# Hybrid encoder trunk, one core: squares, root and convolution gate placed inside the input projection, nine of twelve groups of branch transposes placed inside the linear attention, one gate product placed at its tail

## The chip, the cores and the metric

The kernel runs on one core of one Trainium2 chip. The metric is the device time of one execution in microseconds. The profile that is read below is one execution of the kernel before.

## What is computed

Two layers run over 768 tokens (a group of 512 and one of 256), all float32. Each layer starts with four mixers that share one input projection; then come an expert-choice mixture of experts and a gated input embedding, which the change leaves alone.

```python
def mixer_block(h, w_in, ...):
    u = h @ w_in                                   # 2592 columns for the mixers, 4096 for the gates
    qa = axial_rope(rmsnorm(qa, qk_g[0]), ...); ka = axial_rope(rmsnorm(ka, qk_g[1]), ...)
    oa = global_attention(qa, ka, va)
    ob = conv_module(ub, ...)                      # z = a * sigmoid(g), depthwise convolution, norm, silu
    oc = window_attention(rope(qc), rope(kc), vc, sink)
    od = gla_mixer(qd, kd, vd, rd, zlr, g2, gb2, gn)   # gated linear attention, rmsnorm, * silu(rd)
    gates = sigmoid(gates.reshape(B, S, 4, D_MODEL))
    merged = 0.0
    for i, o in enumerate((oa, ob, oc, od)):
        merged = merged + gates[:, :, i] * (o @ w_branch[i])
    return merged @ w_out
```

## The kernel before

Tokens lie in six tiles of 128. A float32 operand of a product is split into a high part (ScalarE copies it to fp32r: `hi`, `gate_hi`, `t_hi`, lines 714, 724, 746) and a low part (VectorE subtracts: `lo`, `gate_lo`, `t_lo`, lines 997, 1002, 1007), and TensorE makes three products of them. The order on each engine is written out by hand, as one program per engine; engines wait for each other through counting semaphores. Each queue is strictly in order, so a waiting instruction holds back all behind it.

A layer's mixer part runs in these stages.

- **Projection.** Six chunks of 432 columns, four weight steps each (`chunk`, `w_chunk`, lines 1433 to 1435). ScalarE empties a chunk into `u` (line 767) when TensorE has finished it. Chunk 0 holds the queries and keys of the global attention, chunks 1 and 2 the convolution's halves `UB` and `UG`.
- **Gates.** The 4096 gate columns are 32 products of 48 matmuls each (`gate_step`, line 1462), numbered f, which fill TensorE where a mixer would leave it waiting. Each needs its weights loaded (SyncE, line 475), split into `fhi` and `flo`, and its result copied out (`gate_out`, line 732) and stored to `gate_logits` (line 485).
- **Rope.** VectorE squares the queries and keys and sums them (lines 1053, 1055), ScalarE takes the sigmoid of `UG` and the root (795, 797), VectorE multiplies `UB` by it (1059), inverts the root (1076), rotates tile by tile into `rA` (1083 to 1097), GpSimd does the same for the window attention into `rC` (619 to 627). TensorE transposes both (1504), ScalarE copies the result out (807 to 809) and VectorE takes the low parts (`qk_lo`, 1068, 1071). Gate product t stands ahead of tile t's transposes, gate 0 ahead of all. Then the convolution input is transposed (1517).
- **Attention and convolution**, then **linear attention** in two passes over the tiles with a scan between. In the first pass a tile has a transpose of the low-rank columns (1578), products with the decay (1582, 1585), a product with `w2b` (1590), gate product `F_GLA + n`, and the key-value products (1601). In the second it has products 1618, half a gate product, 1630, the other half, 1648 and 1657, and twelve transposes (1669). `s_h[7]` tells that VectorE has masked `att` (1242), `s_h[8]` that 1648/1657 are done.
- **Tail.** The sixth tile's output is normalised (`oss`, `od4`, lines 902, 1280, 1282), then all branch outputs are transposed, twelve groups of four (1415), each group followed by `t_hi` and `t_lo` in two PSUM banks; between the sixth and the seventh group the first four branch weights are split.
- **Branches and merge.** Eight column blocks g, four branch products i each (line 1462 again), the gates' sigmoid on ScalarE (915), the product with it on VectorE (1301), the sum on GpSimd (645 to 651). Product i of block g waits for VectorE's product i of block g-1, which frees its banks.

SyncE's queue around the tail, before: after the last gate store it waits for all stores, loads the eight branch weights (493), waits for the normalised output and loads the gates of blocks 0 and 1 (503). `fout[0]` shares its memory with `raw[3]`, and `fhi`/`flo` share theirs with `raw[4]` to `raw[7]`.

## Time and profile before

| what | value |
|---|---|
| runs | 3266.78, 3263.78, 3262.92 us; median 3263.78 us |
| profiled execution | 3267.64 us, its span 3265.8 us |
| TensorE busy | 2936.4 us, 90% of the span |
| VectorE busy | 1973.6 us, 60% |
| ScalarE busy | 1679.0 us, 51% |
| GpSimd busy | 352.3 us, 11% |
| mean granted TensorE clock | 0.932 of full speed |
| TensorE's share of the chain that ended last | 72% |

The span runs from the first to the last instruction. The granted clock has two levels, 1.2 and 2.4 GHz, so 1.00 means 2.4 GHz throughout. An idle time of an engine, in brackets in a timeline, names who ended it. The two layers are alike: layer 1's projection lies at 51 to 218 us, layer 2's at 1662 to 1834 us.

### The profile page before, as it was taken

What the parts mean: (1) busy time and instruction counts of PE and PEld (TensorE: products, weight loads), DVE (VectorE), ACT (ScalarE), POOL (GpSimd) and SP (SyncE); (2) the same over time, 40 slices, a digit from 0 to 9 for tenths busy, and PEclk for the clock granted to TensorE, in tenths of its full rate; (3) what the DMA queues carried; (4) which work ended last, traced back from release to release, by engine and by line L of the source; (5) the groups of instructions that cost most, each with busy time, mean ns of one, the idle gap of its engine ahead of it and who ended that gap; (6) DMA issues with size and microseconds to landing.
All of it is one profiled execution on the core that took longest, in us unless ns stands there. A gap on an engine that the chain in (4) does not pass through costs nothing.

```text
span 3265.8 us, 45051 instructions
## 1 busy us (share of the span) xinstructions
PE 2936.4 (90%) x15468; PEld 2376.2 (73%) x15468; DVE 1973.6 (60%) x2548; ACT 1679.0 (51%) x2320; POOL 352.3 (11%) x362
## 2 busy tenths in 40 slices
PE   5989989989869999996979899899896999999966
PEld 4988877868746666664779888788685666666655
DVE  2135872447378888885231559533564788888833
ACT  3223335234258888885232333452332788888832
POOL 2012000006001011011010200000240011011010
PEclk9999989979879999997979999899896999999978
DMA  5112112137289999995131121121565899999832
GB/s 190 49 32 85 57 56 69 55 100 244 110 302 373 375 371 373 375 373 172 55 102 33 54 75 57 57 80 38 144 215 194 309 372 373 375 371 373 310 132 86
DMA packets 378229, 617.78 MB, mean 189 GB/s; under 512 B 20448, under 2 KB 141376, under 8 KB 377984
## 3 DMA queue, kind: packets, MB, share of 16 engines
q1 hardware_dynamic: 356080, 539.69, 47.7%
q0 software_dynamic: 20304, 70.21, 7.3%
q10 hardware_dynamic: 1728, 6.29, 0.5%
q8 instruction: 76, 1.25, 0.2%
q14 instruction: 41, 0.34, 0.0%
HBM read 553.20 MB, written 62.91 MB: 189 GB/s over the span
## 4 chain that ended last, share of the span: by engine, by line
PE 72%; ACT 9%; DVE 8%; issue 5%; DVEq 3%; DMA 2%; ACTq 1%; POOL 0%; POOLq 0%
PE PS L1462 18%; PE PS L1433 14%; PE PS L1435 14%; PE PS L1434 13%; ACT whi L714 5%; PE PS L1415 3%; DVE wlo L997 1%; PE PS L1553 1%; DVE zacc L1121 1%; PE PS L1704 1%; ACT L947 1%; ACT L714 1%; PE PS L1648 1%; DVE rows L1019 1%; PE PS L1618 1%
## 5 line engine op out<-in xcount | busy, mean ns | idle before, releaser
L997 DVE TENSOR_TENSOR wlo<-raw,whi 128x1024 fp32r<-128x1024 f32 (+2 forms) x880 | 1024.2, 1206 | 602.8 <-ACT whi L714 596.7
L714 ACT ACTIVATE whi<-raw 128x1024 fp32r<-128x1024 f32 (+2 forms) x880 | 886.2, 1036 | 502.5 <-PE PS L1435 485.7
L1462 PE MATMUL PS<-hT,fhi 128*128 128x512 f32 (+1 forms) x2048 | 460.1, 347 | 13.6 <-ACT fout L732 8.0
L1433 PE MATMUL PS<-whi,xeT 128*96 128x512 f32 x1024 | 411.9, 402 | 12.8 <-DVE wlo L997 10.3
L1435 PE MATMUL PS<-whi,xeT 128*96 128x512 f32 x1024 | 405.4, 396 | 0.0
L1434 PE MATMUL PS<-wlo,xeT 128*96 128x512 f32 x1024 | 403.5, 394 | 0.0
L1433 PE MATMUL PS<-whi,hT 128*128 128x432 f32 (+1 forms) x960 | 362.7, 378 | 17.3 <-DVE rows L1399 9.1
L1462 PEld LDWEIGHTS PS<-hT,fhi 128*128 128x128 f32 x2048 | 324.2, 193 | 73.3 <-issue 27.3
L1434 PE MATMUL PS<-wlo,hT 128*128 128x432 f32 (+1 forms) x960 | 360.1, 375 | 0.0
L1435 PE MATMUL PS<-whi,hT 128*128 128x432 f32 (+1 forms) x960 | 359.9, 375 | 0.0
L1462 PE MATMUL PS<-hT,flo 128*128 128x512 f32 (+1 forms) x1024 | 268.5, 344 | 0.0
L1433 PEld LDWEIGHTS PS<-whi,xeT 128*96 128x96 f32 x1024 | 165.8, 162 | 102.0 <-DVE wlo L997 34.4
L1435 PEld LDWEIGHTS PS<-whi,xeT 128*96 128x96 f32 x1024 | 166.1, 162 | 72.8
L1434 PEld LDWEIGHTS PS<-wlo,xeT 128*96 128x96 f32 x1024 | 166.6, 163 | 66.5
L1433 PEld LDWEIGHTS PS<-whi,hT 128*128 128x128 f32 x960 | 183.8, 191 | 42.6 <-issue 14.3
L1433 PE MATMUL PS<-whi,hidT 128*96 128x512 f32 x512 | 207.4, 405 | 0.0
L1435 PE MATMUL PS<-whi,hidT 128*96 128x512 f32 x512 | 201.5, 394 | 0.0
L1434 PE MATMUL PS<-wlo,hidT 128*96 128x512 f32 x512 | 201.0, 393 | 0.0
L1435 PEld LDWEIGHTS PS<-whi,hT 128*128 128x128 f32 x960 | 183.5, 191 | 20.0
L1434 PEld LDWEIGHTS PS<-wlo,hT 128*128 128x128 f32 x960 | 184.0, 192 | 18.9
L1462 PEld LDWEIGHTS PS<-hT,flo 128*128 128x128 f32 x1024 | 159.7, 192 | 23.4
L832 ACT ACTIVATE P<-PS,nm 128x256 f32<-128x256 f32 (+2 forms) x96 | 54.1, 563 | 177.5 <-DVE nm L1138 95.4
(273 smaller groups left out, 3967.2 us busy)
## 6 DMA issues: line engine op xcount, KB each, us to landing
raw<-in_w_gate_e SPq DMA_DIRECT2D x256, 512.0 KB, 10.5
raw<-in_w_up_e SPq DMA_DIRECT2D x256, 512.0 KB, 10.8
raw<-in_w_down_e SPq DMA_DIRECT2D x256, 512.0 KB, 11.2
raw<-in_w_in SPq DMA_DIRECT2D x64, 512.0 KB, 4.3
raw<-in_w_in SPq DMA_DIRECT2D x48, 432.0 KB, 3.3
rows<-x_res POOLq DMA_DIRECT2D x36, 512.0 KB, 8.3
x_res<-rows POOLq DMA_DIRECT2D x30, 512.0 KB, 4.3
gate_logits<-raw SPq DMA_DIRECT2D x32, 384.0 KB, 2.7
```

The lines of the kernel that those rows point to most:

```text
L714: A(whi[slot % SPLIT][:, 0:w], raw[slot][:, 0:w], ACT.Copy).then_inc(s_hi, 1)
L832: A(P[:, n % 2, 0:nk * 128], PS[:, n % 2, 0:nk * 128], ACT.Exp, bias=nm[:, n:n + 1], accum_out=sm[:, n:n + 1]).then_inc(s_p, 1)
L947: A(sil[:, c * 512:(c + 1) * 512], PS[0:CAP, c, :], ACT.Silu).then_inc(s_sil, 1)
L997: V.tensor_tensor(wlo[j % SPLIT][:, 0:w], raw[j % slots][:, 0:w], whi[j % SPLIT][:, 0:w].bitcast(F32), ALU.subtract).then_inc(s_lo, 1)
L1019: V.scalar_tensor_tensor(rows[:, t, :], rows[:, t, :], rs[:, t:t + 1], gain[:], ALU.mult, ALU.mult).then_inc(s_xn, 1)
L1121: V.scalar_tensor_tensor(zacc[:, c, :], z, cw[:, c, k:k + 1], zacc[:, c, :], ALU.mult, ALU.add).then_inc(s_conv, 1)
L1415: m = nc.tensor.transpose(PS[:, 6 + b, n * np_:(n + 1) * np_], x, ident[0:np_, 0:np_])
L1433: nc.tensor.matmul(out, x[0], w[0], start=first, stop=False)
L1434: nc.tensor.matmul(out, x[0], w[1], start=False, stop=False)
L1435: return nc.tensor.matmul(out, x[1], w[0], start=False, stop=last)
L1462: m = nc.tensor.matmul(PS[:, bb, 0:(t1 - t0) * 128], w[wn], x[xn](t0, t1), start=first and p == 0, stop=last and p == 2)
L1553: mm = nc.tensor.matmul(PS[:, 4 + (m // 4) % 2, h * HD:(h + 1) * HD], PT[:, m % 2, k * 128:(k + 1) * 128], u[:, k0 + k, v0:v0 + HD], start ...
```

## The change

1. The squares and sums of the queries and keys are made by VectorE after chunk 1's weight steps (scratch in `rA`), the root by ScalarE after chunk 1, the sigmoid of `UG` after chunk 2, and the inverse and the product with `UB` by VectorE after chunk 3's steps. The projection loops of ScalarE and VectorE are unrolled for this. TensorE's loop stays.
2. The gate product ahead of the sixth rope tile is left out there. All later products move one number down (`F_Z` is 5), and number 31, `F_TAIL`, is made at the end of the second pass: its first quarter behind 1630 of the last tile, the rest behind the first two transposed groups of the fourth branch.
3. The transposes are grouped anew (`T_UNITS`): six groups `AB` (one tile, two branches), three `C` and three `D` (two tiles, one branch). The nine groups AB and C run in the first pass of the linear attention, one behind the gate product of each tile, a second behind the key-value products of each odd tile, all in PSUM bank 3. The decays' products move from bank 3 to bank 0, behind the product with `w2b`.
4. At the tail the output of tiles 0 to 3 is normalised early (`od_norm(0, 4)`), and three groups are left, in banks 4, 3 and 5.
5. SyncE loads three branch weights and block 0's gates ahead of the last gate store, block 1's gates behind it, and the fourth to eighth branch weights after those.

The diff, cut to its core:

```diff
-F_ROPE, F_Z, F_ATT, F_CONV, F_GLA, F_SCAN, F_GLB = 0, 6, 8, 17, 19, 25, 26
+F_ROPE, F_Z, F_ATT, F_CONV, F_GLA, F_SCAN, F_GLB, F_TAIL = 0, 5, 7, 16, 18, 24, 25, 31
...
 T_N0, T_G, T_N1 = 0, 12, 24
+T_UNITS = [("AB", 0), ("AB", 1), ("C", 0), ("AB", 2), ("AB", 3), ("C", 1), ("AB", 4), ("AB", 5), ("C", 2),
+           ("D", 0), ("D", 1), ("D", 2)]
...
+        def branch_units(n):
+            return [k for k, (kind, m) in enumerate(T_UNITS)
+                    if (kind == "AB" and m == n) or (kind == "C" and 2 * m + 1 == n)]
+        def branch_bank(k):
+            kind, m = T_UNITS[k]
+            return PS[:, (4, 3, 5)[m] if kind == "D" else 3, :].rearrange("p (k n) -> p k n", n=256)
+        def branch_src(k, h):
+            kind, m = T_UNITS[k]
+            if kind == "AB":
+                return [ublk[:, m, b, 0, h * 128:(h + 1) * 128] for b in (0, 1)]
+            return [ublk[:, t, 2 if kind == "C" else 3, 0, h * 128:(h + 1) * 128] for t in (2 * m, 2 * m + 1)]
...
+                def load_branch(g):
+                    sp.wait_ge(s_lo, l * SPL + (S_G + g + 1))
...
+                def load_gates(g):
+                    for i in range(NB):
+                        if g >= 2:
+                            sp.wait_ge((s_mg, s_ga1, s_ga2, s_mg)[i], l * 8 + (g - 1))
+                        sp.dma_start(gates[g % 2][:, i], g_d[g * NB + i].rearrange("p (t n) -> p t n", n=128)
...
+                    if f == NF - 1:
+                        sp.wait_ge(s_flo, l * NF + NF)
+                        for g in range(FRAW):
+                            load_branch(g)
+                        sp.wait_ge(s_fout[0], l * (8 * NF) + 8 * NF)
+                        sp.wait_ge(s_fout[1], l * (8 * NF) + 8 * NF - 16)
+                        sp.wait_ge(s_h[8], l * NT + NT)
+                        load_gates(0)
...
-                wait_alone(sp, s_flo, l * NF + NF)
-                wait_alone(sp, s_fused, l * NF + NF + FSPLIT)
+                sp.wait_ge(s_fused, l * NF + NF + FSPLIT)
+                sp.wait_ge(s_od, 2 * l + 2)
+                load_gates(1)
                 for n in range(2):
-                    wait_alone(sp, s_fout[n], l * (8 * NF) + 8 * NF)
-                for g in range(8):
...
-                for g in range(10):
+                    sp.wait_ge(s_fout[n], l * (8 * NF) + 8 * NF)
+                for g in range(FRAW, 8):
+                    load_branch(g)
+                for g in range(2, 10):
...
-                with act.Fori(0, 2) as i:
-                    for j in range(2):
-                        w_chunk(i * 2 + j, 4 * j, True)
-                w_chunk(4, 0, True)
+                for ck in range(5):
+                    w_chunk(ck, 4 * (ck % 2), True)
+                    if ck == 1:
+                        act.wait_ge(s_ssq, l + 1)
+                        A(rqk[:], rqk[:], ACT.Sqrt, bias=eps64[:]).then_inc(s_rqk, 1)
+                    if ck == 2:
+                        act.drain()
+                        for t in range(NT):
+                            A(u[:, t, UG:UG + 256], u[:, t, UG:UG + 256], ACT.Sigmoid).then_inc(s_zs, 1)
...
-                    A(u[:, t, UG:UG + 256], u[:, t, UG:UG + 256], ACT.Sigmoid).then_inc(s_zs, 1)
-                act.wait_ge(s_ssq, l + 1)
-                A(rqk[:], rqk[:], ACT.Sqrt, bias=eps64[:]).then_inc(s_rqk, 1)
-                for t in range(NT):
-                    gate_hi(l, t + 1)
-                    gate_out(l, t)
+                    if t < NT - 1:
+                        gate_hi(l, t + 1)
+                        gate_out(l, t)
...
+                def branch_hi(k):
+                    t_hi(l * TPL + (T_G + k), branch_dst(k, 1), branch_bank(k))
...
+                        for k in branch_units(n):
+                            branch_hi(k)
...
-                    if t < NT - 1:
-                        gate_hi(l, F_GLB + t + 1)
+                    gate_hi(l, F_GLB + t + 1)
...
-                act.wait_ge(s_oss, l + 1)
-                A(oss[:], oss[:], ACT.Sqrt, bias=eps64[:]).then_inc(s_or, 1)
-                for c in range(2):
-                    if c == 1:
-                        act.wait_ge(s_od, l + 1)
-                        for n in range(4):
-                            hi(l * SPL + (S_G + n), n, 1024, R_G)
-                    for t in range(NT):
-                        t_hi(l * TPL + (T_G + 6 * c + t), urblk[:, t, 2 * c:2 * c + 2, 1, :],
-                             PS[:, 6 + t % 2, :].rearrange("p (k n) -> p k n", n=256))
+                act.wait_ge(s_oss, 2 * l + 1)
+                A(oss[:, 0:4], oss[:, 0:4], ACT.Sqrt, bias=eps64[:]).then_inc(s_or, 1)
+                branch_hi(9)
+                branch_hi(10)
+                act.wait_ge(s_oss, 2 * l + 2)
+                A(oss[:, 4:6], oss[:, 4:6], ACT.Sqrt, bias=eps64[:]).then_inc(s_or, 1)
+                act.wait_ge(s_h[8], l * NT + NT)
+                hi(l * SPL + S_G, 0, 1024, R_G)
+                branch_hi(11)
+                hi(l * SPL + (S_G + 1), 1, 1024, R_G)
+                hi(l * SPL + (S_G + 2), 2, 1024, R_G)
+                gate_out(l, F_TAIL)
+                hi(l * SPL + (S_G + 3), 3, 1024, R_G)
...
-                with dve.Fori(0, NCH // 2) as i:
-                    for j in range(8):
-                        lo(l * SPL + i * 8 + j, j, 2 * CW)
+                for ck in range(NCH):
+                    for n in range(4):
+                        lo(l * SPL + ck * 4 + n, (ck % 2) * 4 + n, 2 * CW)
+                    if ck == 1:
+                        dve.wait_ge(s_ea, l * AAPL + 6 + 6)
+                        for t in range(NT):
+                            x = u[:, t, QA:QA + 384]
+                            sq = rA[:, t % 2, 0:3].rearrange("p h a d -> p (h a d)")
+                            V.tensor_tensor(sq, x, x, ALU.mult)
+                            dve.drain()
+                            V.tensor_reduce(rqk[:, t, :], heads(sq), AX.X, ALU.add)
+                        dve.drain().then_inc(s_ssq, 1)
+                    if ck == 3:
+                        dve.wait_ge(s_rqk, l + 1)
+                        V.reciprocal(rqk[:], rqk[:])
+                        for t in range(NT):
+                            dve.wait_ge(s_zs, l * NT + t + 1)
+                            V.tensor_tensor(u[:, t, UB:UB + 256], u[:, t, UB:UB + 256], u[:, t, UG:UG + 256],
+                                            ALU.mult).then_inc(s_zr, 1)
...
-                    gate_lo(l, t + 1)
+                    if t < NT - 1:
+                        gate_lo(l, t + 1)
...
+                def branch_lo(k):
+                    t_lo(l * TPL + (T_G + k), branch_dst(k, 0), branch_bank(k), branch_dst(k, 1))
...
+                def od_norm(a, b):
+                    V.reciprocal(oss[:, a:b, :], oss[:, a:b, :])
+                    dve.drain()
+                    V.tensor_tensor(od4[:, a:b], od4[:, a:b], oss[:, a:b, :].unsqueeze(3).broadcast_to([128, b - a, 4, HD]),
+                                    ALU.mult).then_inc(s_od, 1)
...
+                        branch_lo(branch_units(n)[0])
...
+                    if n < NT:
+                        for k in branch_units(n)[1:]:
+                            branch_lo(k)
...
+                    if n == NT:
+                        dve.wait_ge(s_or, 2 * l + 1)
+                        od_norm(0, 4)
...
-                        if n < NT - 1:
-                            gate_lo(l, F_GLB + n + 1)
+                        gate_lo(l, F_GLB + n + 1)
...
-                        if n == NT:
+                        if m in (3, NT - 1):
                             dve.drain().then_inc(s_oss, 1)
...
-                for n in range(4):
+                branch_lo(9)
+                branch_lo(10)
+                dve.wait_ge(s_or, 2 * l + 2)
+                od_norm(4, 6)
+                lo(l * SPL + S_G, 0, 1024)
+                branch_lo(11)
+                for n in range(1, 4):
                     lo(l * SPL + (S_G + n), n, 1024)
...
-                    if t > 0:
+                    if 0 < t < NT - 1:
                         gate_step(l, F_ROPE + t)
...
+                def branch_transposes(k):
+                    if k < 9:
+                        pe.wait_ge(s_tlo, l * TLL + (T_G + k + 2))
+                    out = branch_bank(k)
+                    for h in range(2):
+                        for n, x in enumerate(branch_src(k, h)):
+                            mm = nc.tensor.transpose(out[:, n, h * 128:(h + 1) * 128], x, ident)
+                    mm.then_inc(s_tp, 1)
...
+                        if n >= 2:
+                            pe.wait_ge(s_g[6], l * NT + n - 1)
...
+                    if n < NT:
+                        pe.wait_ge(s_g[1], l * NT + n + 1)
+                        nc.tensor.matmul(PS[:, 1, :], zlT[0:33, :], w2b[0:33, :], start=True, stop=True).then_inc(s_g[2], 1)
+                    if n >= 1:
                         for k in range(4):
-                            mm = nc.tensor.matmul(PS[:, 3, 2 * k:2 * k + 2], la[:, m, k * 128:(k + 1) * 128],
+                            mm = nc.tensor.matmul(PS[:, 0, 128 + 2 * k:130 + 2 * k], la[:, m, k * 128:(k + 1) * 128],
...
-                        pe.wait_ge(s_g[1], l * NT + n + 1)
-                        nc.tensor.matmul(PS[:, 1, :], zlT[0:33, :], w2b[0:33, :], start=True, stop=True).then_inc(s_g[2], 1)
                         gate_step(l, F_GLA + n)
+                        branch_transposes(branch_units(n)[0])
...
+                    if n < NT:
+                        for k in branch_units(n)[1:]:
+                            branch_transposes(k)
...
+                    else:
+                        gate_step(l, F_TAIL, 0, 2)
...
-                wait_alone(pe, s_fev, l * NF + NF + 1)
-                for c in range(2):
-                    if c == 1:
-                        wait_alone(pe, s_od, l + 1)
-                    for t in range(NT):
-                        transposes(None, t % 2, [ublk[:, t, 2 * c + k // 2, 0, (k % 2) * 128:(k % 2) * 128 + 128]
-                                                 for k in range(4)], (s_tlo, l * TLL + (T_G + 6 * c + t + 1)))
-                pe.wait_ge(s_tlo, l * TLL + (T_G + 12 + 2))
+                pe.wait_ge(s_od, 2 * l + 1)
+                branch_transposes(9)
+                branch_transposes(10)
+                gate_step(l, F_TAIL, 2, KT)
+                pe.wait_ge(s_od, 2 * l + 2)
+                branch_transposes(11)
...
                         if g >= 1:
                             pe.wait_ge(s_gm[i], l * 8 + g)
+                        elif i < 3:
+                            pe.wait_ge(s_tlo, l * TLL + (T_G + (9, 11, 12)[i] + 2))
+                        else:
+                            pe.wait_ge(s_fev, l * NF + NF + 1)
```

How the change moves instructions, at three places. VectorE at the projection; `wlo` are the weights' low parts, four to a chunk. Before, behind the loop of the projection:

```order
L1042 COMPARE_AND_BRANCH
L1002 TENSOR_TENSOR flo_95<-raw_49,fhi_93 128x1024
L1053 TENSOR_TENSOR s_123<-u 128x384
L1055 TENSOR_REDUCE rqk<-s_123 128x6
...
L1059 TENSOR_TENSOR u<-u 128x256 x6
L1076 RECIPROCAL rqk<-rqk 128x36
L1083 TENSOR_TENSOR s_124<-u,rqk 128x384
```

After the change, from the last weight steps of chunk 1 on, and with the rotation behind the last chunk:

```order
L1048 TENSOR_TENSOR wlo_88<-raw_56,whi_84 128x864
L1101 TENSOR_TENSOR rA<-u 128x384
L1103 TENSOR_REDUCE rqk<-rA 128x6
...
L1048 TENSOR_TENSOR wlo_85<-raw_49,whi_81 128x864
...
L1107 RECIPROCAL rqk<-rqk 128x36
L1110 TENSOR_TENSOR u<-u 128x256 x6
...
L1053 TENSOR_TENSOR flo_95<-raw_49,fhi_93 128x1024
L1137 TENSOR_TENSOR s_124<-u,rqk 128x384
```

The rotation now follows the gate's low part directly.

TensorE in the first pass of the linear attention, from the end of one gate product to the start of the next. Before:

```order
L1462 MATMUL PS<-hT_72,flo_96 128x256
L1601 MATMUL PS<-u,TT 64x64 x16
L1578 MATMUL PS<-cst,u 32x128
L1582 MATMUL PS<-la,cst 128x256 x2
L1585 MATMUL PS<-cst,la 128x2 x4
L1590 MATMUL PS<-w2b,zlT 128x512
```

After, behind an odd tile's gate product:

```order
L1525 MATMUL PS<-hT_72,flo_96 128x256
L1640 MATMUL PS<-cst,u 128x128 x4
L1679 MATMUL PS<-u,E_136 64x64 x16
L1640 MATMUL PS<-cst,u 128x128 x4
L1653 MATMUL PS<-cst,u 32x128
L1657 MATMUL PS<-la,cst 128x256 x2
L1661 MATMUL PS<-w2b,zlT 128x512
L1664 MATMUL PS<-cst,la 128x2 x4
```

Two groups of four transposes have come in (behind an even tile one), and the last two products have changed places.

SyncE's queue at the tail, with the semaphores that it waits for. Before:

```order
L485 DMA gate_logits<-fout_97 128x768 [waits s_fev]
L493 DMA raw_49<-in_w_branch 128x8x128 [waits s_flo,s_cst,s_fused,s_fout0,s_lo,s_fout1]
L493 DMA raw_50<-in_w_branch 128x8x128 [waits s_lo]
...
L503 DMA gates_92<-gate_logits 128x768 [waits s_od] x4
L503 DMA u<-gate_logits 128x6x128 [waits s_od] x4
```

After:

```order
L508 DMA raw_49<-in_w_branch 128x8x128 [waits s_lo,s_flo]
L508 DMA raw_50<-in_w_branch 128x8x128 [waits s_lo]
L508 DMA raw_51<-in_w_branch 128x8x128 [waits s_lo]
L517 DMA gates_92<-gate_logits 128x768 [waits s_h8,s_fout1,s_fout0]
L517 DMA gates_92<-gate_logits 128x768 x3
L534 DMA gate_logits<-fout_97 128x768 [waits s_fev]
L517 DMA u<-gate_logits 128x6x128 [waits s_od,s_fused]
L517 DMA u<-gate_logits 128x6x128 x3
L508 DMA raw_52<-in_w_branch 128x8x128 [waits s_lo,s_fout1,s_fout0]
```

The fourth branch weight (`raw_52`) now stands behind the last gate store and block 1's gates.

## Rows read from the trace of the kernel before

**Rows 1.** Windows: us, busy (instructions) by engine, granted clock, DMA share, GB/s; layer 2.

```profile
2110.00:2183.00 73.00, 73.00 (x498) 59.99 (x499) 17.99 (x25) 40.96 (x57) 0.00 (x0) 0.96 0.24 67
2303.00:2337.00 34.00, 19.91 (x111) 16.09 (x109) 16.69 (x28) 14.89 (x22) 0.00 (x0) 0.65 0.79 214
```

**Rows 2.** Timeline of PE, first rope transposes: start, us, what [idle before <- releaser].

```profile
241.77 1.51 PE L1504 MATMUL PS<-cst,rA 128*128 128x128 f32 x6 [9.95 <-DVEq L1098]
...
1853.59 1.51 PE L1504 MATMUL PS<-cst,rA 128*128 128x128 f32 x6 [10.57 <-DVEq L1098]
...
1864.70 0.82 PE L1504 MATMUL PS<-cst,rA 128*128 128x128 f32 x6
1865.35 0.82 PE L1504 MATMUL PS<-cst,rC 128*128 128x128 f32 x6
```

**Rows 3.** Timeline of DVE and POOL behind layer 2's projection.

```profile
1835.22 1.27 DVE L1053 TENSOR_TENSOR s<-u 128x384 f32<-128x384 f32 x1 [19.53 <-ACT u L767]
...
1843.93 5.73 DVE L1059 TENSOR_TENSOR u<-u 128x256 f32<-128x256 f32 x6
...
1852.46 0.96 DVE L1097 TENSOR_TENSOR rA<-s,s 128x768 f32<-128x768 f32 x1
...
1840.80 1.97 POOL L627 TENSOR_TENSOR rC<-c,c 128x768 f32<-128x768 f32 x1 [3.43 <-issue]
```

**Rows 4.** The chain that ended last, in order of time: start, us, what.

```profile
284.20 8.50 PE PS L1462 x48
...
2337.26 69.19 PE PS L1462 x384
```

**Rows 5.** Timeline of DVE and PE, end of layer 1's rope.

```profile
294.45 0.43 DVE L1068 TENSOR_TENSOR q<-PS,q 64x256 fp32r<-64x256 f32 x1 [4.13 <-ACT ur L809]
...
297.13 1.09 PE L1517 MATMUL PS<-cst,u 128*128 128x128 f32 x4 [3.13 <-issue]
```

**Rows 6.** Timeline of PE, first and second pass of layer 1's linear attention.

```profile
546.80 0.98 PE L1601 MATMUL PS<-u,E 64*64 64x64 f32 x32
...
628.90 0.55 PE L1648 MATMUL PS<-u,att 128*128 128x64 f32 x4
...
633.44 1.50 PE L1669 MATMUL PS<-cst,E 128*128 128x128 f32 x12 [0.71 <-DVEq L1258]
...
651.29 2.46 PE L1669 MATMUL PS<-cst,E 128*128 128x128 f32 x12 [0.71 <-DVEq L1258]
```

**Rows 7.** Timeline of PE, tail of layer 2's linear attention.

```profile
2302.24 1.50 PE L1669 MATMUL PS<-cst,E 128*128 128x128 f32 x12 [0.70 <-DVEq L1258]
2304.94 1.71 PE L1630 MATMUL PS<-TT 64*128 64x128 f32 x16 [1.20 <-ACTq L898]
2308.17 1.11 PE L1648 MATMUL PS<-u,att 128*128 128x64 f32 x4 [1.52 <-DVEq L1243]
...
2314.81 1.97 PE L1415 MATMUL PS<-cst,u 128*128 128x128 f32 x8
...
2337.26 1.13 PE L1462 MATMUL PS<-ur,whi 128*128 128x512 f32 x4 [2.63 <-DVE wlo L997]
```

**Rows 8.** Timeline of ACT and SP, layer 1's tail and merge.

```profile
713.65 3.88 ACT L714 ACTIVATE whi<-raw 128x1024 fp32r<-128x1024 f32 x4
...
723.95 1.28 ACT L915 ACT_TABLE_LOAD   x1
725.24 3.04 ACT L915 ACTIVATE gates<-gates 128x768 f32<-128x768 f32 x4
...
748.87 2.81 SPq L503 DMA_DIRECT2D u<-gate_logits  x4
```

**Rows 9.** DMA issues of the page: count, KB each, median us from issue to landing.

```profile
raw<-in_w_in SPq DMA_DIRECT2D x64, 512.0 KB, 4.3
...
gate_logits<-fout SPq DMA_DIRECT2D x32, 384.0 KB, 2.7
...
raw<-in_w_branch SPq DMA_DIRECT2D x16, 512.0 KB, 7.5
```

52 lines of the change are left out of this document (13 added, 39 removed).

## Prediction

> **What bounds the kernel now.** I read the windows by stage first, then TensorE's timeline at the places the change touches, then the other engines' there. In the first pass of the linear attention TensorE is busy for 73.00 of 73.00 us, so whatever is added to TensorE there is paid for. At the tail it works 19.9 of 34 us at a granted clock of 0.65 [rows 1]. Behind the projection it stands idle for 9.95 us in layer 1 and 10.57 in layer 2, until VectorE's `rA` comes [rows 2]. So the mixer part has two holes per layer, and the change works on both; what it moves goes into a stage without one. Below, layer 2 is reckoned from its rows and layer 1 taken alike where its rows are alike.
>
> **A. Squares, root, sigmoid, product inside the projection.** VectorE starts at 1835.2 and needs until 1849.7 for squares and products, then 3.8 us for inverse and rotation, `rA` being ready at 1853.4 [rows 3]. After the change the rotation is free to start at 1835.2 and ends near 1839, under gate 0, which ends at 1843.0 (10.57 before 1853.59). GpSimd's `rC` ends at 1842.8 and is wanted a little later, so it fits by less than a microsecond. One wait stays: the first transposes wait for gate 0's copy-out of 768 columns, 0.8 us by the sigmoid rows [rows 8]. TensorE also comes back slow from the hole: six transposes take 1.51 us behind it and 0.82 later [rows 2], 1.4 for twelve. Worth: 9.95 - 0.8 + 1.4 = 10.5 and 11.2 us. The moved work costs nothing inside the projection: a chunk is 28.7 us of TensorE (172 us for six), and VectorE's 8.7 us of squares and 5.7 of products [rows 3] start with a chunk, whose successor's first weights are wanted only at its end, some 20 us later. Without that cover each microsecond would be paid. Sum **-21.7 us**; bounds -16 (GpSimd late by up to the 3.43 us for which it stood idle for no reason shown) and -23.
>
> **B. The sixth tile's gate leaves the rope.** Before, gate 5 starts at 284.20 [rows 4], twelve transposes (1.3 us) behind the end of gate 4 at 282.9; the convolution's transposes start at 297.13 [rows 5]: 14.2 us. With the gate gone, a chain lies bare that it hid: the fifth tile's transposes, their copy-out, the low parts (VectorE 1.75 us behind a gate's end at 292.70, all done 4.4 behind it [rows 5]), then the sixth tile's second transposes 0.7, copy-out and low parts 2.8. That is 7.9 us, so 6.3 go per layer, **-12.6**; bounds -10 and -14. The gate's own 8.5 us come back in D.
>
> **C. Nine groups inside the first pass.** Six transposes follow the next six in 0.65 us [rows 2], 0.11 each, so nine groups of four are 3.9 us per layer. In odd tiles the second group needs bank 3, which the first leaves only after gate copy-out 0.8, `t_hi` 0.5, `t_lo` 0.7 and the signals; 1.4 us of it (transposes 0.4, key-value products 0.98 [rows 6]) is covered, 0.75 is bare, three times. 3.9 + 2.3 = 6.2 per layer. ScalarE's and VectorE's share hides: they work 41 and 18 of 73 us there [rows 1]. In the second pass a wait of 0.71 us sometimes came with a slow spell, 2.46 us in place of 1.50 for twelve transposes [rows 6]; with what follows it such a spell costs 1.7 us, and I put one on the six new waits. Sum **+14.1**; bounds +8 (no waits) and +23 (a slow spell at each of the six waits, or transposes at 0.25 us throughout, as at the slow tail, where eight take 1.97 us [rows 7]).
>
> By the Trainium skill (TensorE: Matmul & The Clock Gate, Part 4) a 128x128 transpose costs about 275 ns in a kernel's context; 36 would then be 9.9 us per layer and C 12 us dearer. The rows here have 108 ns per transpose in a row of six, so the trace does not bear it out; it is the fifth case below.
>
> **D. The tail.** Counted from 2302.24, the start of the last twelve transposes; the first branch product now starts 35.0 us later and the eight blocks take 69.2 [rows 4, 7], together 104.2. After: product 1630 ends at 4.4. The first quarter of `F_TAIL` (2.1 us) fills the 1.52 of waiting for the mask, to 6.5. Products 1648/1657 take 3.8 us at full speed (628.90 to 632.7 [rows 6]) and 6.6 in the tail [rows 7]; I take 3.8, since a gate stands before them: 10.3. Eight transposes 0.9, the other 36 matmuls of the gate 6.4, four transposes 0.4: 18.0. Block 0's products run until 26.5, but block 1's wait for block 0's sigmoids, and here is what is late next. ScalarE's queue is: `t_hi` 0.5, two weights' high parts at 0.97, gate copy-out 0.8, to 21.4. Only then does SyncE store gate 31, issue four loads (2.8 us [rows 8]), and load the fourth branch weight, which lands 7.5 us after issue [rows 9]: 31.9; the store itself is down after 2.7 [rows 9] and holds up nothing. ScalarE stands before that weight's high part with the sigmoids queued behind: 1.0, table load 1.3, sigmoid 0.8 [rows 8], VectorE's product 0.96 (as `rA`, the same size [rows 3]): block 1 starts at 35.9. Seven blocks at 69.2/8 are 60.5, the end is at 96.4. That is 7.8 us less, with gate 31 paid, in layer 1 alike: **-15.6**. Bounds: the weight lands 4.3 us after issue, as the projection's do [rows 9], and gate 31's copy-out comes 2.5 us earlier, -27; the clock stays low to the end of the gate (+9) and the products of block 1 start slow, 0.
>
> **Sum.** -21.7 - 12.6 + 14.1 - 15.6 = -35.8 us. The profiled execution took 3267.64 us (span 3265.8), 3.9 above the median of 3263.78; the 35.8 taken from the median give **3228 us**. A measurement of this kernel can tell about 0.2% (6.5 us) from no change.
>
> **Rivals.**
> 1. The tail gives nothing. For it: the chain from gate 31's copy-out through SyncE to the fourth weight is 14.5 us long, the queue is strictly in order, and each microsecond in it is one of the stage. Against: it would have to be 7.8 us longer. 3228 + 15.6 = 3244.
> 2. The tail gives more: the fourth weight lands early and TensorE's clock comes up. The bound of D, 11 more, is 3217.
> 3. The clock falls in the first pass (slower). Place: the first pass, now at 0.96 over its 73 us without a gap [rows 1]; the three new waits per layer are as long as the 0.71 us that came with a slow spell [rows 6]. Price: at half speed, work that takes 1 us takes 2. The gain is 17.9 us per layer, so it turns into a loss from some 18 us of full-speed work per layer done slow, a quarter of the stage; all of it would be +73 per layer, and half of it, 3228 + 73 = 3301. Against: in the second pass, with a wait of that length at every tile, most tiles ran fast.
> 4. The change does not do what it says at the projection: squares ahead of chunk 2's first weights in VectorE's queue hold up the next chunk. Were it so, it would show at two of the five joints, and the 8.7 us of squares would be paid in each layer: 3245. Against: the 20 us of room.
> 5. Transposes are dear in the first pass, as slow as at the tail: 36 x (0.25 - 0.11) is 5 us per layer: 3238. At the price of the skill's page it would be 3240.
>
> **Chances.** Forecast with its own bounds 0.52 (3221 to 3236), more at the tail 0.15, nothing at the tail 0.13, dear transposes 0.08, projection held up 0.04, clock falls 0.04, and 0.04 for the rope's gain lost together with the tail's, 3228 + 21.7 + 15.6 = 3265. From 3213 to 3245 leaves out about 2 in 10: deep in rival 2, and rivals 3 and 4. Slower by over 0.2% is rival 3, 0.04; within 0.2% is most of the last case, 0.03; faster is the rest, 0.93.
>
> **What would show it.** A: no idle time over 1 us before the first rope transposes, and no new wait of the projection's products for `wlo`. B: two idle times of 1.5 to 3 us before the last rope and the convolution's transposes. C: the first pass at about 79 us, TensorE idle 0.7 us at odd tiles. D: the first branch product some 18 us behind the start of the last twelve transposes, then one idle time of about 9 us before block 1, ended by VectorE's product, behind ScalarE's wait for a load of `raw`. Wrong it would be if TensorE's idle time before block 1 is over 15 us, if the first pass takes over 85 us, or if the projection grows.

## The result, and the profile of the changed kernel

The changed kernel takes **3248.72 us** (median of 6 runs, 3243.85 to 3253.67) against 3264.64 for the kernel before (6 runs, 3262.92 to 3266.78): ratio 0.9952, 95% interval 0.9939 to 0.9964. It is faster by 16 us where 36 were forecast, outside the range of 3213 to 3245. The profiled execution has a span of 3250.9 us, 14.9 less than before.

To see where the forecast and the trace part, I cut both traces at the same places of TensorE's timeline: the start of the linear attention (the first transpose of `zl`), the start of the last twelve transposes (L1752 after, L1669 before), the start of the last group of products with a weight's low part in the last block, the first router product, the gather's first transpose and the expert's last transpose of `sil`. us, layer 1 and layer 2:

| stretch | before | after | change | forecast |
|---|---|---|---|---|
| up to the linear attention | 494.8, 618.1 | 475.7, 601.2 | -36.0 | A + B -34.3 |
| its two passes | 193.8, 196.4 | 204.1, 204.1 | +17.9 | C +14.1 |
| tail and eight blocks | 106.4, 103.7 | 103.7, 103.9 | -2.5 | D -15.6 |
| router, first product to gather | 56.1, 55.5 | 58.5, 58.7 | +5.5 | 0 |
| all the rest | | | +0.2 | 0 |

A, B and C are near their sizes; the tail gives back almost nothing, and the router stage, which the change doesn't touch, got longer. TensorE's timeline in layer 1, at the places of A, B and C:

```profile
231.68 0.85 PE L1567 MATMUL PS<-cst,rA 128*128 128x128 f32 x6 [0.95 <-issue]
...
274.97 0.84 PE L1567 MATMUL PS<-cst,rA 128*128 128x128 f32 x6 [2.61 <-DVE klA L1128]
276.27 0.85 PE L1567 MATMUL PS<-cst,rC 128*128 128x128 f32 x6 [0.46 <-DVE klC L1128]
279.56 0.63 PE L1580 MATMUL PS<-cst,u 128*128 128x128 f32 x4 [2.44 <-issue]
...
507.30 0.66 PE L1640 MATMUL PS<-cst,u 128*128 128x128 f32 x4 [0.77 <-DVE ur L1058]
534.71 0.66 PE L1640 MATMUL PS<-cst,u 128*128 128x128 f32 x4 [0.77 <-DVE ur L1058]
561.97 0.66 PE L1640 MATMUL PS<-cst,u 128*128 128x128 f32 x4 [0.77 <-DVE ur L1058]
```

The hole of 9.95 us before the first rope transposes [rows 2] is down to 0.95, and the six transposes behind it take 0.85 us instead of 1.51. The last tile's chain lies bare as forecast (2.61, 0.46 and 2.44 us). The three odd tiles of the first pass each wait 0.77 us for bank 3. Now the tail of layer 1, against [rows 7]; the last two lines are from block 1:

```profile
679.82 2.45 PE L1752 MATMUL PS<-cst,E 128*128 128x128 f32 x12 [0.70 <-DVEq L1332]
683.47 3.09 PE L1711 MATMUL PS<-TT 64*128 64x128 f32 x16 [1.20 <-ACTq L946]
...
690.48 0.56 PE L1731 MATMUL PS<-u,att 128*128 128x64 f32 x4
...
694.46 1.97 PE L1640 MATMUL PS<-cst,u 128*128 128x128 f32 x8
...
697.75 0.87 PE L1525 MATMUL PS<-hT,fhi 128*128 128x512 f32 x4
...
703.40 0.95 PE L1525 MATMUL PS<-ur,whi 128*128 128x512 f32 x4
...
722.17 1.62 PE L1525 MATMUL PS<-ur,whi 128*128 128x512 f32 x4 [10.09 <-DVE gates L1364]
...
728.03 0.87 PE L1525 MATMUL PS<-ur,whi 128*128 128x512 f32 x4
```

The chain that ended last, through the same wait (start, us, what), where [rows 4] had eight blocks in one piece:

```profile
706.18 0.70 ACT fout L773
707.32 0.63 SPq L517
...
710.48 7.33 DMA raw<-in_w_branch
717.83 1.06 ACT whi L755
718.90 1.28 ACT L966
720.20 0.85 ACT gates L966
721.07 0.96 DVE gates L1364
722.17 61.86 PE PS L1525 x336
```

Every link forecast is there: gate 31's copy-out, four loads of gates, the fourth weight, its high part, table load, sigmoid, product. From copy-out to block 1 it takes 16.0 us (15.3 forecast). But it starts 26.4 us after the last twelve transposes, not 20.6, since TensorE works at half clock from 679.82 until shortly before 697.75: twelve transposes in 2.45 us, not 1.50, and sixteen products in 3.09, not 1.71. Windows (us, busy by engine, granted clock, DMA share, GB/s), the first pass, the tail, blocks 1 to 7, the router stage, against [rows 1]:

```profile
495.00:567.00 72.00, 67.87 (x538) 55.89 (x537) 22.60 (x34) 41.04 (x60) 0.00 (x0) 0.98 0.24 71
682.00:722.00 40.00, 28.89 (x166) 24.93 (x164) 15.56 (x26) 12.35 (x17) 0.00 (x0) 0.76 0.56 158
722.00:784.00 62.00, 61.83 (x337) 53.93 (x338) 51.77 (x43) 35.70 (x44) 45.69 (x22) 0.95 0.70 222
858.00:917.00 59.00, 29.19 (x140) 28.20 (x138) 25.00 (x60) 10.81 (x21) 1.89 (x4) 0.50 0.64 237
```

### The profile page after: what moved, and what is told of

Same layout as the page of the kernel before. It is cut to its first block, busy times and chain, and to the rows that moved or that the text cites. A ratio compares the mean times of both kernels' runs of the same rounds, so it can differ in the third digit from the quotient of the medians.

```text
span 3250.9 us, 44867 instructions
## 1 busy us (share of the span) xinstructions
PE 2936.1 (90%) x15468; PEld 2376.1 (73%) x15468; DVE 1978.4 (61%) x2552; ACT 1676.4 (52%) x2320; POOL 356.3 (11%) x362
## 3 DMA queue, kind: packets, MB, share of 16 engines
q8 instruction: 76, 1.25, 0.2%
## 4 chain that ended last, share of the span: by engine, by line
PE 70%; ACT 10%; DVE 9%; issue 5%; DVEq 3%; DMA 2%; ACTq 1%; POOL 0%; SPq 0%; POOLq 0%
PE PS L1525 16%; PE PS L1496 14%; PE PS L1498 14%; PE PS L1497 14%; ACT whi L755 5%; PE PS L1478 3%; DVE wlo L1048 1%; PE PS L1616 1%; PE PS L1789 1%; DVE zacc L1176 1%; ACT L998 1%; ACT L755 1%; PE PS L1731 1%; DVE rows L1070 1%; PE PS L1752 1%
## 5 line engine op out<-in xcount | busy, mean ns | idle before, releaser
L1525 PEld LDWEIGHTS PS<-hT,fhi 128*128 128x128 f32 x2048 | 328.1, 195 | 67.2 <-issue 20.5
L1478 PE MATMUL PS<-cst,rows 128*128 128x128 f32 x288 | 69.9, 424 | 85.8 <-DVE rows L1070 69.9
## 6 DMA issues: line engine op xcount, KB each, us to landing
raw<-in_w_up_e SPq DMA_DIRECT2D x256, 512.0 KB, 10.1
```

The costliest lines, as they stand in the source:

```text
L1478: m = nc.tensor.transpose(PS[:, 6 + b, n * np_:(n + 1) * np_], x, ident[0:np_, 0:np_])
L1525: m = nc.tensor.matmul(PS[:, bb, 0:(t1 - t0) * 128], w[wn], x[xn](t0, t1), start=first and p == 0, stop=last and p == 2)
```

## Experiments

Each median is of four to six executions, taken beside the kernel before on the same chip. The theory after the result is that block 1's wait of 10 us for a weight that it does not need is the tail's price. Its rivals are that the tail is held by the clock, or by the transfers themselves. All medians come first, then each run.

| run | median us | ratio to before | 95% interval |
|---|---|---|---|
| e2, A alone | 3239.1 | 0.9924 | 0.9910 to 0.9937 |
| e5, changed kernel again | 3248.0 | 0.9946 | 0.9931 to 0.9960 |
| e4, tail gate undone | 3244.9 | 0.9942 | 0.9928 to 0.9956 |
| e8, fill | 3236.2 | 0.9915 | 0.9902 to 0.9928 |
| e9, order | 3225.5 | 0.9887 | 0.9872 to 0.9902 |
| e6, tail gate undone, weight early | 3221.5 | 0.9868 | 0.9853 to 0.9884 |
| e1, weight early | 3219.0 | 0.9864 | 0.9849 to 0.9879 |
| e3, nine groups in the tail | 3218.5 | 0.9870 | 0.9853 to 0.9887 |
| e10, six groups in the pass | 3209.7 | 0.9832 | 0.9819 to 0.9846 |
| e7 and e11, spread | 3205.9, 3206.1 | 0.9829, 0.9832 | 0.9816 to 0.9848 |

And the stages of their profiled executions, cut as above (us, layer 1 / layer 2; "to block 0" is from the last twelve transposes to the first branch product, "blocks" from there to the last group):

```
run        passes         to block 0     blocks         router
before     193.8 / 196.4  37.4 / 35.0    69.1 / 68.7    56.1 / 55.5
e2         193.5 / 194.3  34.8 / 36.5    68.7 / 69.2    55.6 / 55.5
after      204.1 / 204.1  23.6 / 23.5    80.1 / 80.4    58.5 / 58.7
e5         203.9 / 203.9  21.9 / 17.8    79.0 / 80.2    58.6 / 58.5
e8         203.8 / 203.8  20.2 / 17.4    80.0 / 80.2    52.9 / 58.7
e4         203.9 / 203.8  20.8 / 20.7    76.1 / 76.4    52.8 / 58.7
e6         203.6 / 204.5  20.6 / 19.9    68.9 / 68.7    55.5 / 52.8
e1         203.8 / 204.1  17.9 / 23.6    67.1 / 67.2    58.7 / 58.7
e9         203.9 / 203.9  23.6 / 17.9    68.7 / 68.4    55.9 / 52.7
e3         196.8 / 194.0  29.7 / 28.3    67.1 / 67.1    55.6 / 55.6
e10        200.1 / 200.2  19.1 / 20.8    67.1 / 67.1    55.4 / 58.8
e7         197.4 / 196.8  20.7 / 21.1    71.8 / 71.8    52.9 / 52.7
e11        194.1 / 196.5  20.9 / 19.6    71.8 / 71.8    52.5 / 58.6
```

**e1, the weight early.** In SyncE's part:

```diff
                         sp.wait_ge(s_fout[0], l * (8 * NF) + 8 * NF)
+                        load_branch(FRAW)
                         sp.wait_ge(s_fout[1], l * (8 * NF) + 8 * NF - 16)
...
-                for g in range(FRAW, 8):
+                for g in range(FRAW + 1, 8):
                     load_branch(g)
```

> The changed kernel with the load of the fourth branch weight ahead of the loads of the first gates, instead of behind the store of gate 31. Theory (the tail's price is a wait of block 1 for that weight: 10.09 us in layer 1, 10.50 in layer 2, at the first gate product of VectorE): the wait goes to some 1 us, 2 x 9 = 18 us off the changed kernel's 3248.7, 3230. Rival (the tail is held by the slow clock at its start, the wait is cover for something else, say the gates' loads): under 6 us off, 3243 to 3248.

3219.0 us, 29 below the changed kernel. Its layer 1, SyncE, then ScalarE:

```profile
676.46 4.46 SPq L508 DMA_DIRECT2D raw<-in_w_branch  x4
689.94 1.76 SPq L517 DMA_DIRECT2D gates<-gate_logits  x4
700.94 0.32 SPq L535 DMA_DIRECT2D gate_logits<-fout  x1
```

```profile
700.11 0.80 ACT L774 ACTIVATE fout<-PS 128x768 f32<-128x768 f32 x1
700.80 1.06 ACT L756 ACTIVATE whi<-raw 128x1024 fp32r<-128x1024 f32 x1
701.88 1.28 ACT L967 ACT_TABLE_LOAD   x1
703.18 3.05 ACT L967 ACTIVATE gates<-gates 128x768 f32<-128x768 f32 x4
```

The fourth weight leaves with the first three, the sigmoids start while block 0 still runs, and TensorE has no idle time at all before block 1. I had expected 18 us, the two waits. The blocks went from 80.1 and 80.4 to 67.1 and 67.2, 13.0 and 13.2 each: behind a wait of 10 us TensorE starts at half clock (1.62 us for four matmuls in the row at 722.17, 0.86 at full clock), and that costs 2.8 more per layer: the eighteen matmuls from 722.17 to 728.03 take 5.86 us, and three times six at full clock some 3.2. Twice 13.1 is 26 of the 29; the rest is no more than the clock varies elsewhere.

**e9, only the order in the queues.** Is it the transfer, or what stands behind it? The load stays late, but its split is queued behind the sigmoids and products that block 1 needs. ScalarE's half of the edit is shown; the weight's low part moves on VectorE in the same way.

```diff
-                hi(l * SPL + (S_G + 3), 3, 1024, R_G)
                 for g in range(9):
...
                             A(gates[g % 2][:, i], gates[g % 2][:, i], ACT.Sigmoid).then_inc(s_sg, 1)
+                    if g == 0:
+                        hi(l * SPL + (S_G + 3), 3, 1024, R_G)
```

> The changed kernel, the fourth weight as late as the change has it, but its split (high part on ScalarE, low part on VectorE) behind the first block's four sigmoids and products instead of ahead of them; TensorE needs that weight three blocks later. Theory (block 1 does not need the weight, it waits because the split stands ahead of the sigmoids in ScalarE's and VectorE's queues): the wait of 10 us falls to 1 or 2, and the 2.8 us of half clock behind it go too; 18 to 24 us off the changed kernel, 3224 to 3230. Rival (the early load in the first experiment helped by taking its transfer out of the way of the gates' loads): under 6 us off.

3225.5 us, 23 below the changed kernel. The weight is as late as ever (ScalarE, layer 1), and TensorE's wait is 1.33 us and further on:

```profile
709.46 3.05 ACT L965 ACTIVATE gates<-gates 128x768 f32<-128x768 f32 x4
719.78 1.06 ACT L755 ACTIVATE whi<-raw 128x1024 fp32r<-128x1024 f32 x1 [7.26 <-DMA raw<-in_w_branch]
720.74 3.03 ACT L965 ACTIVATE u<-u 128x768 f32<-128x768 f32 x4
```

```profile
723.10 0.95 PE L1528 MATMUL PS<-ur,whi 128*128 128x512 f32 x4 [1.33 <-DVE u L1365]
```

So it was the order. The load is as late as in the changed kernel and the wait of 10 us is gone all the same; the blocks take 68.7 and 68.4 us instead of 80.1 and 80.4, which is the 23 us. The rival of the transfers falls for these. The early load is 6.5 us better still by the medians; 2.8 of that are the blocks, which take 67.1 and 67.2 there and have no wait at all.

**e3, the nine groups into the tail.** They leave the first pass and stand behind the tail gate's last products, which now go first; banks 0 and 1 in turn. ScalarE copies the tail gate's result out ahead of all groups, so the edit changes two things. TensorE's and then ScalarE's part:

```diff
-                        branch_transposes(branch_units(n)[0])
...
+                gate_step(l, F_TAIL, 2, KT)
+                for k in range(9):
+                    branch_transposes(k)
                 pe.wait_ge(s_od, 2 * l + 1)
                 branch_transposes(9)
                 branch_transposes(10)
-                gate_step(l, F_TAIL, 2, KT)
...
                 hi(l * SPL + S_G, 0, 1024, R_G)
-                branch_hi(11)
+                gate_out(l, F_TAIL)
+                for k in range(12):
+                    branch_hi(k)
                 hi(l * SPL + (S_G + 1), 1, 1024, R_G)
                 hi(l * SPL + (S_G + 2), 2, 1024, R_G)
-                gate_out(l, F_TAIL)
```

> The changed kernel with the nine groups of transposes taken out of the linear attention's first pass and put into the tail, behind the tail gate's last products and ahead of the three groups of the last branch; the weight's load where the change has it. Theory (the wait of 10 us in block 1 is slack in which the nine groups fit, and in the first pass they cost 8.5 us a layer): first pass 8.5 us shorter, the first block's products start at about 33 us after the last twelve transposes instead of 23.6, block 1 still at about 42 to 43 us; 16 us off the changed kernel, 3233. Rival (a group costs over 1.2 us in the tail, with ScalarE's and VectorE's copies in a row, or the clock takes it): 3242 to 3250.

3218.5 us, 30 below the changed kernel: more than the 16 expected. The passes are 7.3 and 10.1 us shorter. The groups cost about 1.03 us each in the tail, bound by the copies on ScalarE and VectorE:

```profile
693.48 1.25 PE L1632 MATMUL PS<-cst,u 128*128 128x128 f32 x8 [1.24 <-DVE ur L1055]
695.55 1.25 PE L1632 MATMUL PS<-cst,u 128*128 128x128 f32 x8 [0.82 <-DVE ur L1055]
```

Block 0 starts 5 to 6 us later than in the changed kernel, at 28.3 and 29.7. Block 1 starts not at 42 but without a wait, at about 38 in layer 1, since the tail gate's copy-out no longer stands behind two weights' splits and the groups. Here too the half clock behind the wait went with it.

**e2, A alone,** on the kernel before: squares, root, sigmoids and product moved, the rest left.

```diff
+                    if ck == 1:
+                        act.wait_ge(s_ssq, l + 1)
+                        A(rqk[:], rqk[:], ACT.Sqrt, bias=eps64[:]).then_inc(s_rqk, 1)
+                    if ck == 2:
+                        act.drain()
+                        for t in range(NT):
+                            A(u[:, t, UG:UG + 256], u[:, t, UG:UG + 256], ACT.Sigmoid).then_inc(s_zs, 1)
```

> The kernel before with the squares, the root, the sigmoids and the conv gate's products moved into the projection, and nothing else. Theory (the first step of the forecast was right by itself, and rope and tail lost 34 us together): 21.7 us off the kernel before, 3243. Rival (the sum of 34 was right by luck and this part is worth what a clock state makes of it): 12 or less, or over 28.

3239.1 us, 25.4 below the kernel before. Up to the linear attention it is 11.6 us in layer 1 and 11.5 in layer 2. The first step of the forecast, 21.7, holds by itself, a little low. A alone beats the whole change by 9 us.

**e4 and e6, the tail gate undone.** Old numbering of the gates, gate 5 back in the rope, none in the tail; e4 with the weight's load as changed, e6 with it early.

```diff
-                    if 0 < t < NT - 1:
+                    if t > 0:
                         gate_step(l, F_ROPE + t)
...
-                gate_step(l, F_TAIL, 2, KT)
```

> The changed kernel with the sixth tile's gate back in the rope stage and no gate in the tail; squares and transposes stay as changed. Theory (the tail gate ends the store, and with it the fourth weight's load, late): rope 6.3 us longer a layer, block 1 at about 32 us after the last twelve transposes instead of 42.4, so 4 us a layer shorter, 3240. Rival (the fourth weight waits for something else than the tail gate's store): rope 6.3 us longer and nothing back but the gate's own products, 3250 to 3261.

> No tail gate (the sixth tile's gate back in the rope stage) and the fourth weight's load early. Theory (the tail gate costs nothing but its own products once the weight is early, and takes 6 us a layer out of rope): slower than the changed kernel with the early weight (3219) by 2 x 6.3 less what the tail gets back, 10.7 us of the gate's products no longer stand in the tail but gate 31 now ends in the pass, so by 0 to 13 us; likeliest 3229. Rival (gate placed here or there is the same): 3219.

3244.9 and 3221.5 us, where 3240 and 3229 were the likeliest. In e4 the part from the rope's first transposes to the first scores is 75.9 us in both layers, against 70.4 and 71.4 with the gate gone; the tail with its blocks is 96.8 and 97.1, against 98.0 to 103.9 in the four layers of the changed kernel. Block 1 starts 35.4 us after the last twelve transposes (expected 32: the load still stands behind four loads of gates that wait for `s_od`). So B's gain in the rope is paid back in the tail, and as built B is worth nothing that shows. Beside the early weight it is 2.5 us by the medians, with overlapping intervals. In the two profiles e6 is 10.0 us behind e1 up to the linear attention, 2.3 behind in tail and blocks, and 9.1 ahead in the router stages, which neither edit touches. Whether B pays beside the early weight stays open.

**e5, the changed kernel again.**

> The changed kernel itself, once more, beside the others of this set. Theory (the tail's waits are of the program, the slow spell at the end of the second pass is of the execution): the median again at 3244 to 3254 with a spread of 6 to 10 us; in the profile the wait of block 1 again 10.1 and 10.5 us, first branch product 18 to 24 us after the last twelve transposes, as the clock has it. Rival (the spell is of the program too): 23.6 and 23.5 us again.

3248.0, spread 14 us. Block 1's wait came back in both layers, 9.46 and 10.69 us. The half clock at the end of the second pass did not: there in layer 1, absent in layer 2, of the same program:

```profile
682.36 2.47 PE L1752 MATMUL PS<-cst,E 128*128 128x128 f32 x12 [0.70 <-DVEq L1332]
...
2286.05 1.50 PE L1752 MATMUL PS<-cst,E 128*128 128x128 f32 x12 [0.70 <-DVEq L1332]
2288.75 1.71 PE L1711 MATMUL PS<-TT 64*128 64x128 f32 x16 [1.20 <-ACTq L946]
```

In layer 2 the first branch product comes at 17.8 us; the forecast said 18.0. Tail and blocks together take 98.0 us there, 5.7 less than in the kernel before, where the forecast had 7.8.

**e8, fill.** One k step of the tail gate goes ahead of the wait of 1.20 us.

```diff
+                    if n == NT:
+                        gate_step(l, F_TAIL, 0, 1)
                     if n >= 1:
                         pe.wait_ge(s_h[4], l * NT + n)
```

> The changed kernel with the first k step of the tail gate ahead of the wait for ScalarE in front of the last score products (1.20 us idle), nothing else. Theory (the slow spell that held the first branch product back by 5.6 us begins at the two idle pieces of 0.70 and 1.20 us there): 1.1 us a layer directly and up to 5 more where the clock stays up, 3239 to 3246. Rival (the spell comes from elsewhere, and the wait for the weight takes whatever is gained ahead of it): within 3 us of the changed kernel.

3236.2 us, 12 below, with intervals apart from the changed kernel's. They are more than the wait filled, 1.2 us a layer, can give. In its profile, beside e5's of the same set, the first branch product comes 1.7 and 0.4 us earlier and the blocks give 1.0 back. Layer 1 still had the slow spell (2.33 us for the twelve transposes). 6.3 of the 13.8 us between the two profiles lie up to the linear attention and 5.5 in the router stages, where the edit changes nothing. So the theory, that the spell begins at this wait, is not shown, and where the rest comes from stays open.

**e10, e7 and e11: groups in the pass or out of it.** e10 leaves one group per tile in the pass and moves the third branch's three groups to the tail, with the early weight. e7, and e11 which is the same kernel, take all nine out and spread them between the tail gate's k steps and block 0's products, with e1's load and e8's fill.

```diff
+                for kk, ks in ((2, (2,)), (3, (3,)), (4, ()), (5, (4,)), (6, (5,)), (7, (6,))):
+                    gate_step(l, F_TAIL, kk, kk + 1)
+                    for k in ks:
+                        branch_transposes(k)
```

> The changed kernel with the fourth weight early, the six groups of the first two branches left in the first pass (one a tile), and the third branch's three groups moved to the tail. Theory (a tile with one group costs 0.54 us in the pass, one with two 1.9): the two passes together some 4 us shorter a layer than with nine, and 3 x 0.45 longer in the tail: 2 x 2.7 below the early weight alone (3219), 3213 to 3216. Rival (the passes' 9 us are the clock's, and go only when all nine are out): 3218 to 3222.

> The changed kernel with the fourth weight early, the nine groups out of the first pass and, with the last three, spread between the tail gate's k steps and the first block's products, two banks in turn; one k step of the tail gate fills the wait ahead of the last score products. Theory (groups in the pass cost 8.5 us a layer; spread in the tail each costs its 0.45 us of TensorE): 4 us of transposes instead of 8.5, and 1.1 us of the wait filled, 2 x 5.6 below the early weight alone (3219): 3208. Rival (what the tail's path gains the clock or the copies on ScalarE and VectorE take): 3216 or more.

> The spread kernel once more. Theory (its lead over the early weight alone is of the program: passes 7 us a layer shorter, tail 5 longer, and the rest the clock of the router stage): median 3204 to 3212, passes again 197 us a layer; router stage 52.8, 55.5 or 58.6 us as the clock has it. Rival (its 52.8 twice was of the program): 52.8 twice again.

3209.7, 3205.9 and 3206.1 us; e10 came 3 us below its range, the other two as expected. The passes take 195.4 us with no group in them (mean of ten layers, 193.5 to 197.4), 200.2 with six, 203.9 with nine (fourteen layers, 203.6 to 204.5): 0.8 us for each of the six, 1.25 for each second group. Spread, a group between the k steps of the tail gate costs little more than its transposes, but four groups in block 0 bring waits (us of e7's layer 1):

```profile
687.44 0.60 PE L1643 MATMUL PS<-cst,u 128*128 128x128 f32 x4
687.79 0.95 PE L1528 MATMUL PS<-hT,fhi 128*128 128x512 f32 x4
...
703.06 0.97 PE L1528 MATMUL PS<-ur,whi 128*128 128x512 f32 x4 [1.41 <-DVE ur L1062]
...
708.41 0.94 PE L1528 MATMUL PS<-ur,whi 128*128 128x512 f32 x4 [0.88 <-DVE gates L1367]
```

It is 0.35 us from the start of the first row to that of the second. The blocks take 71.8 us, 4.7 more than in e1. Against e1 the tail with its blocks is 4.6 us a layer longer (means of four and two layers) for nine groups more, the filled wait set against them: 0.5 us a group. The spread kernel has the lowest median, 1.7% below the kernel before and 1.3% below the changed one, but its interval overlaps that of e10, so which of the two is better isn't shown. Its router stage came at 52.9, 52.7, 52.5 and 58.6, so that was not the program's. It weighs in the comparison, too: of the 12.9 us by which e7's profile is ahead of e1's 11.8 are the router stages, of e11's 12.7 us 6.3.

## Why the prediction was wrong

**A and B** were near together: -34.3 forecast, -36.0 in the profile. Up to the linear attention the nine profiled kernels that have both take 476.6 and 601.9 us (means), the three without B 481.4 and 607.1, the kernel before 494.8 and 618.1: A is 24.4 us (21.7 forecast), B 10.0 (12.6). That the sum fits so well is luck, as the two misses cancel. In B the chain laid bare takes 8.7 us from the end of the rope's last gate (270.89 in layer 1) to the convolution's transposes (279.56), where 7.9 was reckoned. Where A's extra 2.7 us come from stays open.

**C** was forecast at 14.1 and measures 17.9 in the profile, 17.2 by the means above. Its waits are as forecast, 0.77 us three times. Of its terms the group itself was too cheap: the third tile, with one group, takes 13.04 us from gate to gate (510.83 to 523.87) where it took 12.5, so 0.54 instead of 0.43. And a slow spell of 1.5 us came in each layer where I had put one of 1.7 in both together (layer 1's second tile took 15.89 us where the fourth, with the same work, took 14.37). At 275 ns for a transpose, the price that the Trainium skill states (TensorE: Matmul & The Clock Gate, Part 4), nine groups would by estimate be 9.9 us a layer, nearer to the 8.6 measured than my 7.05. But its price per transpose is not what the rows show (four in 0.66 us at full clock); the sum is made of transposes, waits and clock.

**D** is the step that failed: -15.6 forecast, -2.5 measured in the profile, so 13.1 of the 20.9 us missed. The chain was right link by link, and "one idle time of about 9 us before block 1" came at 10.09 and 10.50. The term that was mis-sized is above all the start of the tail, "18.0", and by the clock. I had product 1630 "at 4.4", the gate's first quarter at 2.1 and eight transposes at 0.9, by full-clock rows of layer 2, and took "layer 1 alike". In the changed kernel's layer 1 product 1630 is done at 6.7, the quarter takes 4.0 and the eight transposes 1.6. Products 1648/1657 took 4.0 us where I had chosen 3.8, so that choice was right. The profile of before already showed 2.21 us for the same twelve transposes of layer 1 and 3.09 for the products of 1630.

Within the second pass it is a matter of which tiles the slow spells meet: of the six rows of twelve transposes, one to a tile, the second and the fifth are slow in the kernel before's layer 2 (2.79 and 2.35 us), the second, fourth and sixth in both layers of the changed kernel (2.38 to 2.79), and the sixth begins the tail. Of the changed kernel's four profiled layers three began the tail at half clock; there the first branch product comes at 21.9 to 23.6 us, not 18.0, and as all that follows is one chain, the delay goes through to the end. In the fourth it comes at 17.8, and there 5.7 of the 7.8 us forecast are gained.

A smaller part is the seven blocks, put at 69.2/8 each, 60.5, which took 61.86. That was an average over blocks of mixed clock; at full clock the blocks take 67.1 (e1), 58.8 for seven, and the 10 us of idle time ahead cost some 3 more. In layer 1 of the changed kernel the late start makes 5.8 us, the chain 0.7 and the blocks 1.4, together 7.9, and in layer 2 about as much. Against that stands the kernel before's layer 1, which was 2.7 us longer there than the layer 2 that I reckoned from: twice 7.9 less 2.7 is 13.1. What I had set as bound for this case, "0", was near the truth, and I gave it too little. The sign that I had named, a wait of over 15 us before block 1, did not come: it watched the wait, not the start.

There is also an omission in the reasoning. I found the wait and left it as part of the sum; I did not ask whether block 1 needs what it waits for. It does not, as e9 shows: the weight belongs to the fourth block. The wait with its half clock is 26 us of the program. It was in the forecast, so it is not what the forecast missed, but it is what the change left to gain.

**The router stage** was forecast at 0 and gave +5.5. TensorE's timeline there, before and then after, layer 2:

```profile
2480.95 1.98 PE L1704 MATMUL PS<-wr,hTf 128*128 128x16 f32 x16
...
2483.69 2.58 PE L1704 MATMUL PS<-wr,hTf 128*128 128x16 f32 x16
```

```profile
2463.27 3.43 PE L1789 MATMUL PS<-wr,hTf 128*128 128x16 f32 x16
...
2468.29 3.43 PE L1789 MATMUL PS<-wr,hTf 128*128 128x16 f32 x16
```

The same sixteen products take 1.98 and 2.58 us, or 3.43: a tile is 2.7 us or 5.0. Depending on when the clock falls the stage is 52.5 to 52.9, 55.4 to 56.1, or 58.5 to 58.8 us. The changed kernel had 58.6 in all four profiled layers and the kernels with its parts had all three values; within six of them (e4, e6, e8, e9, e10, e11) the two layers differ. So no edit tried sets it, and what does stays open, as no experiment was made on it alone. The medians above contain it: a difference of some 6 us between two kernels can be a router stage.

**The rivals.** Rival 1, a tail that gives nothing, is what happened in size (3244 against 3248.7), by the clock and not by a chain 7.8 us longer. Rival 3, a clock fall in the first pass, did not happen: 0.98 over 72 us. Rival 4 did not either: the first rope transposes came 10 us earlier. Rival 2 had the fourth weight landing 4.3 us after issue; it took 7.3 and 6.1 us, against 7.5 reckoned. Rival 5, every transpose in the first pass at 0.25 us, is excluded by four in 0.66 us.

## To carry to other kernels

When a load or a split is queued in order ahead of work that doesn't need it, the wait is the whole of the chain behind the load; ask of each link of a late chain whether the waiting stage uses it. A wait of TensorE of some 10 us costs more than its length, here 13 instead of 10. And work moved into a stage without a gap costs its full price (0.8 to 1.25 us per group of four transposes here). Spread over a stage where the copying engines have time, nine groups came to 0.5 us each; packed one behind the other there, to 1.03.

## What I had not expected of the hardware

One program's stages take one of a few lengths, by the granted clock: the start of the tail 17.8, 21.9 or 23.6 us in the changed kernel, the router stage 52.7, 55.6 or 58.6, and this from layer to layer within one execution. The changed kernel's twelve runs spread over 16 us, the kernel before's over 11 in all sets. A forecast from one profiled layer takes such a level for the program's.
